# Two small index tables of a two-block transformer kernel change places in on-chip memory

## The reference

```
x = x + y;  x = x + squared_relu_mlp(rms_norm(x, norm_mlp[i]), mlp_w_up[i], mlp_w_down[i])   # block 1, per layer
merged = sigmoid(gate_ssd) * y_ssd + sigmoid(gate_mla) * y_mla                               # block 2
h = h + merged @ w_o[i]
h = h + memory_cross_attention(rms_norm_2(h, norm_xattn[i]), rms_norm_2(mem, norm_mem[i]), ...)
h = h + hierarchical_moe(rms_norm_2(h, norm_moe[i]), ...)    # 32 experts: (silu(t@gate) * (t@up)) @ down, top 2
return rms_norm_2(h, norm_final)
```

## Time and profile before

| | us |
|---|---|
| median of 3 runs (1234.28 to 1236.28) | 1235.14 |
| the profiled execution | 1234.28 |
| its span, first to last instruction | 1232.5 |
| PE busy | 1179.9 (96%) |
| DVE busy | 783.6 (64%) |
| ACT busy | 608.3 (49%) |

### The profile page before, as it was taken

One profiled execution on the slowest core, in us unless ns is written; L12 is line 12 of the kernel. 1 busy time (PEld: TensorE's weight loads), 2 busy tenths in 40 slices (PEclk: granted clock), 3 DMA queues, 4 the chain that ended last, 5 costly groups with the idle time before them and its releaser, 6 DMA issues. The chain is left out here.

```text
span 1232.5 us, 22410 instructions
## 1 busy us (share of the span) xinstructions
PE 1179.9 (96%) x9056; PEld 1000.1 (81%) x9056; DVE 783.6 (64%) x1316; ACT 608.3 (49%) x993; POOL 100.0 (8%) x102
## 2 busy tenths in 40 slices
PE   9999999999999999999999989999999999999992
PEld 7989999999999999899999988899999833333320
DVE  6876655566755566999899889879655552221213
ACT  6665554455544554767655576665554331111101
POOL 0000100000200000000000030010100004341301
PEclk9999999999999999999999999999999999999997
DMA  9654566564456656445444384365543999999993
GB/s 303 203 172 137 189 189 198 185 196 146 162 181 195 193 182 197 137 152 173 155 137 138 109 274 139 104 205 168 186 160 124 421 360 412 417 413 414 412 404 130
DMA packets 161045, 270.28 MB, mean 219 GB/s; under 512 B 17625, under 2 KB 126142, under 8 KB 156862
## 3 DMA queue, kind: packets, MB, share of 16 engines
q1 hardware_dynamic: 149872, 260.53, 60.6%
q0 software_dynamic: 10720, 8.42, 2.3%
q10 hardware_dynamic: 366, 0.12, 0.0%
HBM read 287.89 MB, written 13.63 MB: 245 GB/s over the span
## 5 line engine op out<-in xcount | busy, mean ns | idle before, releaser
L2128 DVE TENSOR_TENSOR weights_parts<-ring,weights_parts 128x1024 fp32r<-128x1024 f32 (+3 forms) x312 | 363.5, 1185 | 138.4 <-ACT weights_parts L1546 138.0
L1546 ACT ACTIVATE weights_parts<-ring 128x1024 fp32r<-128x1024 f32 (+3 forms) x312 | 309.1, 1011 | 144.6 <-PE psum L885 143.9
L883 PE MATMUL psum<-xnorm_parts,weights_parts 128*128 128x256 f32 x852 | 243.4, 286 | 6.8 <-DVE arena L2531 3.2
L884 PE MATMUL psum<-xnorm_parts,weights_parts 128*128 128x256 f32 x852 | 237.5, 279 | 0.0
L885 PE MATMUL psum<-xnorm_parts,weights_parts 128*128 128x256 f32 x852 | 237.5, 279 | 0.0
L883 PE MATMUL psum<-expert_cols,weights_parts 128*128 128x256 f32 (+1 forms) x688 | 192.5, 280 | 3.5 <-DVE expert_cols L2146 2.2
L884 PE MATMUL psum<-expert_cols,weights_parts 128*128 128x256 f32 (+1 forms) x688 | 190.1, 276 | 0.0
L885 PE MATMUL psum<-expert_cols,weights_parts 128*128 128x256 f32 (+1 forms) x688 | 190.1, 276 | 0.0
L883 PE MATMUL psum<-hidden_parts,weights_parts 128*128 128x256 f32 x640 | 178.7, 279 | 3.0 <-DVE hidden_parts L2599 1.7
L884 PE MATMUL psum<-hidden_parts,weights_parts 128*128 128x256 f32 x640 | 177.1, 277 | 0.0
L885 PE MATMUL psum<-hidden_parts,weights_parts 128*128 128x256 f32 x640 | 177.1, 277 | 0.0
(11 more groups left out here) (452 smaller groups left out, 1723.8 us busy)
## 6 DMA issues: line engine op xcount, KB each, us to landing
ring<-in_mlp_w_up SPq DMA_DIRECT2D x32, 1024.0 KB, 5.4
ring<-in_mlp_w_down SPq DMA_DIRECT2D x32, 1024.0 KB, 4.8
ring<-in_w_in SPq DMA_DIRECT2D x30, 1024.0 KB, 5.1
ring<-in_attn_w_qkv SPq DMA_DIRECT2D x12, 1024.0 KB, 6.0
expert_raw<-in_w_exp_gate SPq DMA_DIRECT2D x22, 512.0 KB
expert_raw<-in_w_exp_up SPq DMA_DIRECT2D x22, 512.0 KB
ring<-in_w_exp_down SPq DMA_DIRECT2D x9, 1024.0 KB
expert_raw<-in_w_exp_down SPq DMA_DIRECT2D x9, 1024.0 KB
```

What stands on the lines that cost most here:

```text
L883: pe.matmul(out, lh, rh, start=start, stop=False, **more)
L884: pe.matmul(out, lh, rl, start=False, stop=False, **more)
L1546: ins = act.activation(high, src, ACT.Copy)
L2128: ins = dve.tensor_tensor(low, src, high.bitcast(F32), ALU.subtract)
```

## The change

The declarations of `half_rows` (128 partitions by 16 integers, 64 bytes in each) and `slot_rows` (by 20 integers, 80 bytes, 96 when rounded up) change places. Each now has the place in the list that is near the other's:

```diff
         arena_rest = sb("arena_rest", [P, ARENA - M_END])
-        half_rows = sb("half_rows", [P, 2, 2 * MORE], I32)
+        slot_rows = sb("slot_rows", [P, NB], I32)
         with nc.sbuf_tensor("expert_weights", [P, 2 * UNITS * UNIT], F32) as w_plain:
             pass
         w_parts = sb("weights_parts", [P, 2 * UNITS * UNIT], F32R)
...
         place_ids = sb("place_ids", [P, 4], I32)
-        slot_rows = sb("slot_rows", [P, NB], I32)
         window_ids = sb("window_ids", [1, SLOTS_ALL], I32)
         more_rows = sb("more_rows", [P, 2 * MORE], I32)
+        half_rows = sb("half_rows", [P, 2, 2 * MORE], I32)
```

## The result

| | before | after |
|---|---|---|
| median of 4 runs, us | 1235.14 (1234.28 to 1236.28) | 1252.23 (1250.96 to 1254.8) |
| ratio, 95% interval | | 1.0151 (1.0132 to 1.0171) |
| span of the profiled execution, us | 1232.5 | 1251.0 |
| PE busy, us | 1179.9 | 1204.6 |

The range forecast was 1231 to 1247, with no change as the likeliest. The time lies above it. Each ratio in this document is the recorded comparison with runs of the kernel before taken beside the kernel in question; it is not the quotient of the two medians. The kernel before itself spreads more than its first four runs show: of its 57 runs beside the three later groups of kernels, 34 lie at 1232.8 to 1236.6 us and 23 at 1238.5 to 1249.5. The 22 runs of the changed kernel on record lie at 1250.4 to 1257.9, above all of them.

What follows compares the result with a forecast made beforehand. Matmuls were taken to bound the dense stages and transfers the expert stage's end. All terms were 0 on the profiled 1234.28 us, so the median was forecast again at 1235.1 us; range 1231 to 1247.

Steps and rivals of the forecast that it cites:

- What bounds each stage: Dense stages last as long as TensorE's matmuls; transfers set the expert stage's end, with 2.5 us of TensorE waiting left.
- Transfers into `expert_weights`, r = 0: Expert stage: transfers to the new address are slower by share r, costing 43.2 r us; r taken as 0, +0 us.
- its rival (1246 us): Expert stage: transfers into expert_weights lose speed at remainder 32, r = 1/4, 10.8 us; chance 0.13.
- The reads of `weights_parts`: Dense stages: TensorE's matmuls reading the moved tensor keep their pace; taken as 0, bounds +10.3 and -14.8 us.
- The row that stood for a matmul at a remainder of 32: Router matmuls reading router_w at remainders 0, 16, 32 and 48: median 279 ns is also the longest, so no extra cost.
- TensorE keeps the slower of its two paces longer: Rival, dense stages: matmuls from 60 to 560 us go to 119.2 ns, +10.3 us, 1245 us; chance 0.05.
- Writers, tables and small tensors, each 0: VectorE and ScalarE writes of weights_parts, and GpSimd's row-number reads (0.07 us either way), were each taken as 0.
- The row for the writers: A VectorE copy with its start read at run time: 19 take 420 to 429 ns, so start does not matter within 2%.

Runs made afterwards that it cites:

- dense_view_32: Kernel before, weights_parts declared 64 bytes larger and used from its byte 32, expert_weights at its old address: 1257.0 us (1.0162).
- the sweep: Measuring kernel, TensorE alone on zeros, 30 stretches of 192 matmuls differing only in operand addresses: 113.8 ns a matmul at distance 64, 119.0 at 96.
- pad_behind: Kernel before with 32 unused bytes behind weights_parts, moving only the small tensors and tables behind it: 1239.0 us (1.0022).
- all_up_64: Kernel before with 64 unused bytes in front of expert_rows and xnorm_parts, so moving tensors and weights_parts all move up by 64: 1239.3 us (1.001).
- all_up_32: Kernel before with 32 unused bytes in front of expert_rows and xnorm_parts, weights_parts at the changed kernel's address, distance still 64: 1238.6 us (1.0032).

## Why the prediction was wrong, step by step

**What bounds each stage: right.** The dense stages last as long as TensorE's matmuls; all the lost time is there, and 24.7 us of busy time became 18.5 us of span. The transfers set the end of the expert stage, and their last waits stayed within 0.3 us.

**Transfers into `expert_weights`, r = 0: right**, and its rival (1246 us) wrong. The stage took 220.0 us for 219.7 at 414 GB/s, and `dense_view_32`, which leaves that tile where it was, lost at least as much as the change.

**The reads of `weights_parts`: this step failed.** It said: "Both stretches read `weights_parts` at the same address, so the address is not what sets them apart here", and took 0. The first half holds, the conclusion does not. Two paces at one address show that something else matters too; they do not show that the address has no part. In the runs, distances of 0, 96, 128 and 192 never reached the steady 113 ns in the sweep, and at 64 both paces occur. The kernel before lived off a distance that allows the fast one; the change took that away, and the term put at 0 measured 24.7 us of busy time.

**The row that stood for a matmul at a remainder of 32: wrong kind of row.** The router's matmuls stream 36 columns behind a load of 128, and start 110 to 112 ns apart within their groups of eight, about as far apart as the fast dense ones that stream 256. So the 36 columns do not set their pace, and a slower read of them could hide. And I looked at the remainder of one operand, where the runs show the difference of two.

**The price: too small even as a rival.** "TensorE keeps the slower of its two paces longer" was the right place at 0.05, with +10.3 us. That sum slowed only the 4182 matmuls from 60 to 560 us, by 2.5 ns each, and held the 119.2 ns of one short stretch against the mean of a long one that has slow parts and waits of its own. Those matmuls slowed by 4.0 ns (116.7 to 120.7, up to 400 us) and 4.4, and the ones behind them by 2.0. Its mechanism was not quite the one found either: it had the kernel stay longer at a pace that it already knew, while at a distance of 96 the fast pace is gone and the steady paces are 117.3 and 118.7 ns, in the first and second MLP of the changed kernel. The time of 1252 lies outside the range because this rival was priced at 1245.

**Writers, tables and small tensors, each 0: right** (1184 and 1010 ns; `pad_behind`). The row for the writers was a weak one all the same: the copy of the earlier trace rows shifts only what VectorE reads, while the change moved what it writes.

| distance by 256 | pace in a sweep, ns | kernels at it, us (ratio to the kernel before beside it) |
|---|---|---|
| 0 | 120 | 1262.8 (1.0214) |
| 52 | 114 | 1233.5 (0.996) |
| 64 | 114, or 118 | 1235.1 (before); 1239.0 (1.0022), 1239.3 (1.001), 1238.6 (1.0032), 1240.8 (1.0027) |
| 76 | 114 | 1232.8 (0.9981) |
| 96 | 119 | 1252.2 (the change, 1.0151); 1255.4 (1.0148), 1257.0 (1.0162) |
| 128 | 119 | 1258.6 (1.0185) |
| 192 | 118 | 1252.2 (1.0122) |

Shown is that the distance decides whether the fast pace is had at all, and that in the sweeps a pace is held once it has settled, some ten to twenty matmuls into a stretch. What picks the pace at a distance of 64 is shown only in part. What in TensorE or the memory makes the loaded and the streamed operand disturb each other is not shown; an account by shared parts of the memory was only argued, and the paces at 48 and 80 do not fit the simple one of 64-byte pieces.

## What to carry to other kernels

A declaration can move a tensor that it does not name: list the start of every operand of the busiest engine before and after an edit, and look at the difference between the two operands that TensorE reads at the same time, not only at remainders of each. Where a profile shows two paces for the same instruction, count it as a sign that placement or timing is worth an experiment of one spacer, and never as proof that placement is free. A sweep kernel that runs one stretch per address settles in one run what a dozen kernels would only suggest; where two paces occur at one address, it needs several starts at each.

## What the runs showed of the hardware

TensorE alone, with 128 columns loaded and 256 streamed in float32 parts, goes at 113.8 to 120.4 ns by the distance of its two operands by 256 bytes, up to 6%. "SBUF — State Buffer" of the Trainium skill, section "SBUF: two separate sides", says that within the engines' side only the pair of ports that GpSimd shares makes for contention and that TensorE never waits on anyone. In the sweep's stretches no other engine works, and nothing but the two addresses differs between them, and they still have these paces. So that sentence does not promise one pace: what costs time here comes with TensorE's own two reads, and there the measurement decides.

Transfers did show a small price of their own, in the two kernels where most tiles of the expert stage left a multiple of 256. In `all_up_64` (its dense pace, then the stage) the rate was 410 GB/s and in `all_up_32` 409, against 414 or 415 over 180 us of the stage in all eleven others, the kernels before and after the change among them:

```profile
190.00:210.00 20.00, 20.00 (x179) 20.00 (x178) 10.81 (x11) 9.40 (x12) 0.00 (x0) 1.00 0.65 210
1015.00:1195.00 180.00, 180.00 (x834) 59.75 (x834) 40.49 (x95) 26.79 (x50) 55.92 (x56) 1.00 1.03 410
```

Two remainders, 32 and 64, and one price of about 1%. "DMA: Bandwidth & Descriptors" of the Trainium skill, section "How a descriptor splits into AXI transactions", says of reads that the unused bytes below the start cost beats. Carried over to these writes, mostly packets of 4096 bytes, it gives an estimate of 0.8% for a remainder of 32 and 1.6% for 64. The size agrees with the trace; that both cost the same does not. With one tile of five it stayed below what 9 us windows could show.
